# Second feed-forward pass of a hybrid pool/mLSTM block: another order of the seven products of a tile

## The chip, the cores and the metric

The kernel runs on one core of a Trainium2 chip, in one launch. The metric is the device time of the whole program in microseconds (us), lower is better. The engines are TensorE (PE), VectorE (DVE), ScalarE (ACT), GpSimd (POOL) and the DMA queue of SyncE (SP). Each works through its own list of instructions in order, and they meet at semaphores.

## The reference, cut to what matters

The reference computes two layers on an image stream x (1024 tokens in a grid of 16 x 64, width 1024) and a context stream (256 tokens). Layer 0 mixes by pooling, layer 1 by an mLSTM. The part that the change touches is the feed-forward network of layer 1 on x:

```
fx = _conv_ffn(_modulate(x, norm_g[i, 2], sh2, sc2), ffn_w_in[i], ...)

def _conv_ffn(h, w_in, conv_w, conv_b, w_out, grid):
    u, g = jnp.split(h @ w_in, 2, axis=-1)      # 1024 -> 2 x 2816
    g = _dwconv_grid(g, conv_w, conv_b, grid)   # depthwise 3x3 on the grid
    return (jax.nn.silu(g) * u) @ w_out         # 2816 -> 1024
```

Everything is float32. A product is made of three matmuls on a high and a low part of each operand (high x high, low x high, high x low).

## The kernel before, in words

The hidden width of 2816 is cut into 22 tiles of 128 channels. For a tile the kernel needs the gate g and the value u, each 128 channels x 1024 tokens, which are held as two halves of 512 tokens. The input has 1024 channels, which are two halves as well. Computed directly that is 8 block products. From tile 2 on the kernel does it with 7, by sums and differences of weight parts (`s1` to `s4`, made by POOL) and of input parts (`t1` to `t4`, made once, before tile 2). Tiles 0 and 1 are computed directly (`plain`).

A block product (`product`, L1364) is 4 x 3 matmuls of 128 x 512. Its result goes to one PSUM bank (L123): `g1`, `s2`, `s3`, `u2` go to bank A, `s1` and `s4` to bank B, `g2` to bank C. Only `g1`, `g2` and `s1` clear their bank; the others add to what stands there, after another engine has read the state in between:

- ACT copies bank A after `g1` (`keep_a`, L2217), bank B after `s1` (into `fprod`, L2222), bank A after `s2` (`keep_b`, L2225) and bank A after `u2` (into `fprod`, L2195).
- DVE adds for the gate's first half (`gate_first_half`, L2896, needs `g2`), for its second half (`gate_second`, L2882, needs `s4`) and for the value's second half (`up_second`, L2888, reads bank A after `s3`). `u2` adds to bank A after this read.

The order of the seven products on PE, and of the weight parts that ACT and POOL make for them, is `ORDER` (L118): g1, s1, s2, s4, s3, g2, u2. Tile 2 ("third") and tile 21 ("last") use `GATE_FIRST` (L117) instead. Behind the products of tile j PE computes `down` (L1463) of tile j-1: 48 matmuls of 128 x 512 with the output weights, which DVE adds into `y_x` (`f_add`, L2912).

On DVE a tile is `f_tile` (L2915): 8 taps of the convolution of tile j-1 (`f_taps`, L2859), `gate_second(j)`, the product of gate and value of tile j-1 (`f_gate`, L2867, needs ACT's silu, L2200), `up_second(j)`, `gate_first_half(j)`, `f_add(j-1)`. Tiles 3 to 12 run in a hardware loop, 13 to 20 are written out. In tiles 14 to 19 (`mod_half`) DVE also computes a piece of the modulation of layer 1, in two parts of two instructions each (`last_mod_part`, L2368 and L2371): one part behind `up_second`, one behind `gate_first_half`. They read `modh` and `macc_x` in SBUF and write `macc_x`.

Each weight part has a high half made by ACT (`part_high`, L2080, in a tile's list on ACT for the next tile) and a low half made by POOL (`part_low`, L3112). POOL also makes the sums of weight parts (`part_sum`, L3102), the low half of the output weights (`out_low`, L3118; high half `out_high`, L2092) and the low half of the gated values (`gated_low`, L3123; high half `gated_high`, L2207). The weights of tile j+1 arrive by one DMA (`halves_in`, L686), which SP issues when all seven low halves of tile j are made.

Ahead of tile 2 lies a start-up. PE computes the plain tiles 0 and 1 (L1381), first for the tokens 0 to 511 and then for 512 to 1023. Meanwhile DVE normalizes the second token half (`pre_half`, L2538 and L2546, which makes the low halves of x12 and x22), and POOL makes `out_low(0)` and then the values and low halves of `t1` to `t4` (L3143) with the weight parts of tile 2 between them.

Of the kernel before, what the change touches and what calls it, by code (L numbers as in the profile page):

```python
# [108 lines left out]
KH = KT // 2  # L109
# [7 lines left out]
GATE_FIRST = ("g1", "g2", "s1", "s2", "s4", "s3", "u2")  # L117
ORDER = ("g1", "s1", "s2", "s4", "s3", "g2", "u2")  # L118
MADE_THIRD = ("s1", "g1", "g2", "u2", "s2", "s4", "s3")
# [7 lines left out]
SUM_STEPS = (11, 12, 14, 15, 17, 18, 20, 21)  # L127
PLAIN_UP = ((1, 1), (5, 4))
THIRD_SLOT = {"g1": "g1", "g2": "g2", "u2": "u2", "s1": "s4", "s4": "s1", "s2": "s3", "s3": "s2"}
# [27 lines left out]
def build(nc, a):  # L157
    with ExitStack() as ctx:
# [351 lines left out]
        def _(sp):  # L510
# [193 lines left out]
            out_in(0)  # L704
            sp.wait_ge(sem("c_shifted"), SECOND["c_shifted"] + 4)
            sp.wait_ge(sem("pool_low"), SECOND["pool_low"] + 2)
# [27 lines left out]
        def _(pe):  # L734
# [685 lines left out]
            def third_first():  # L1420

                pe.wait_ge(sem("act_moved"), 2 * 4 + SECOND["act_moved"])
                pe.wait_ge(sem("tap_done"), SECOND["tap_done"] + 8)
                for name in ("g1", "g2"):
                    product(name, 2 * 7 + (SECOND["lo_in"] + made_at(True, name)), True)

            def products(j, third=False, last=False):
# [12 lines left out]
                if last:  # L1440
                    pe.wait_ge(sem("mod1_done"), FT)
                    product("g2", made("g2"))
                pe.wait_ge(sem("dve_moved"), j * 3 + (summed - 2))
                if third:
# [11 lines left out]
                product("s3", made("s3"), third)  # L1456
                if not (third or last):
                    pe.wait_ge(sem("dve_moved"), j * 3 + summed)
                    product("g2", made("g2"))
                pe.wait_ge(sem("dve_moved"), j * 3 + (summed + (3 if third or last else 2)))  # L1460
                product("u2", made("u2"), third)
# [17 lines left out]
            third_first()  # L1479
            pe.wait_ge(sem("act_moved"), PLAIN_MOVED + 3)  # L1480
            down(0, 0, True)
# [57 lines left out]
        def _(act):  # L1539
# [604 lines left out]
            for d in range(KT):  # L2144
                keep(posts["x_mlstm"], 3, d)
                if d == 3:
                    plain_moved(0, 0)
            half_deviation("q", 3)
            part_high("s1", 2, True)
            for d in range(KH):  # L2150
                high1(d)
            plain_moved(1, 0)
            act.wait_ge(sem("x_out1"), 32 * KT)
            for k in range(KH):
                high1(KH + k)
                act.activation(x12_at[:, k, :], res_h[:, k, :], ACT.Identity, bias=shift(1, 1, "x", k)).then_inc(sem("c_shifted"), 1)
            out_high(0)
            for k in range(KH):
                act.wait_ge(sem("pre_lo"), lows["x_pre2b"] + 12 + k + 1)
                act.activation(x22_at[:, k, :], x22_at[:, k, :], ACT.Identity, bias=shift(1, 1, "x", KH + k)).then_inc(sem("c_shifted"), 1)  # L2160
            plain_moved(0, 1)
            plain_gate(0)
            for k in (0, 2):
                act.wait_ge(sem("pool_low"), SECOND["pool_low"] + 1 + k // 2)
                pair_high("t1", k, x_val["t1"])
            for name in ("g1", "g2", "u2"):
                part_high(name, 2, True)
            for k in range(KH):
                act.activation(x21_at[:, k, :], x21_at[:, k, :], ACT.Identity, bias=shift(1, 1, "x", KH + k)).then_inc(sem("c_shifted"), 1)
            for k in (0, 2):  # L2170
                act.wait_ge(sem("pool_low"), SECOND["pool_low"] + 3 + k // 2)
                pair_high("t2", k, x_val["t2"])
            act.wait_ge(sem("tap_done"), SECOND["tap_done"] + 8)
            act.activation(acc[:], acc[:], ACT.Silu).then_inc(sem("silu_done"), 1)
            plain_moved(1, 1)
            act.wait_ge(sem("a_done"), SECOND["a_done"] + 1)
            act.activation(fa_hi[:], fprod[:, 0, :], ACT.Copy).then_inc(sem("a_hi_ready"), 1)
            for k in (0, 2):
                act.wait_ge(sem("pool_low"), SECOND["pool_low"] + 5 + k // 2)
                pair_high("t4", k, x21_at)  # L2180
            for k in (0, 2):
                act.wait_ge(sem("pool_low"), SECOND["pool_low"] + 7 + k // 2)
                pair_high("t3", k, x_val["t3"])
            plain_gate(1)
            for name in ("s2", "s4", "s3"):
                part_high(name, 2, True)

            def finish(j, par, gate_first=False):

                cv = fcv[:, j + FT, :]  # L2190
                act.wait_ge(sem("dve_moved"), j * 3 + (SECOND["dve_moved"] + (2 if gate_first else 3)))
                act.wait_ge(sem("a_done"), j + SECOND["a_done"])
                act.activation(acc[:], bank(BANK_G, TX), ACT.Identity, bias=cv[:, 9:10], scale=cv[:, 4:5]).then_inc(sem("acc_ready"), 1)
                act.wait_ge(sem("w_in_used"), j * 7 + (SECOND["w_in_used"] + 7))
                act.activation(fprod[:, par, 0:TH], ps[:, BANK_A, :], ACT.Copy).then_inc(sem("act_moved"), 1)  # L2195
# [13 lines left out]
            def tile(j, par, gate_first=False, last=False):  # L2209

                def done(name):

                    act.wait_ge(sem("w_in_used"), j * 7 + (SECOND["w_in_used"] + done_at(gate_first, name)))

                done("g1")
                act.wait_ge(sem("dve_moved"), j * 3 + SECOND["dve_moved"])
                act.activation(keep_a[:], ps[:, BANK_A, :], ACT.Copy).then_inc(sem("act_moved"), 1)  # L2217
                if not last:
                    part_high("g1", j + 1)
                out_high(j - 1)  # L2220
                done("s1")
                act.activation(fprod[:, par, TH:TX], ps[:, BANK_B, :], ACT.Copy).then_inc(sem("act_moved"), 1)  # L2222
                done("s2")
                act.wait_ge(sem("dve_moved"), j * 3 + (SECOND["dve_moved"] - 2))
                act.activation(keep_b[:], ps[:, BANK_A, :], ACT.Copy).then_inc(sem("act_moved"), 1)  # L2225
                if not last:
                    part_high("s1", j + 1)
# [7 lines left out]
                if not last:  # L2235
                    for name in ("s3", "g2", "u2"):
                        part_high(name, j + 1)
# [19 lines left out]
        def _(dve):  # L2257
# [657 lines left out]
            def f_tile(j, par, mod_half=None):  # L2915

                f_taps(j - 1)
                gate_second(j)
                f_gate(j - 1, 1 - par)
                up_second(j, par)  # L2920
                if mod_half is not None:
                    last_mod_part(mod_half, 0)
                gate_first_half(j)
                if mod_half is not None:
# [71 lines left out]
        def _(pool):  # L2996
# [128 lines left out]
            def parts(j, par):  # L3125

                part_low("g1", j)
                out_low(j - 2)
                part_sum("s1", j)
                part_sum("s2", j)  # L3130
# [6 lines left out]
                part_low("s3", j)  # L3137
                part_low("g2", j)
                part_low("u2", j)
# [17 lines left out]
            for k in (0, 2):  # L3157
                pool.wait_ge(sem("pool_low"), SECOND["pool_low"] + 1 + k // 2)
                pool.wait_ge(sem("c_shifted"), SECOND["c_shifted"] + 4 + k + 2)
                moved(x_val["t2"][:, k:k + 2, :], x22_at[:, k:k + 2], x_val["t1"][:, k:k + 2, :])  # L3160
# [130 lines left out]
```

## Time and profile before

| what | value |
|---|---|
| median of 3 runs | 2462.0 us (2458.42 to 2465.99) |
| the profiled execution's own time | 2460.98 us |
| its span | 2459.0 us |
| mean granted TensorE clock | 0.983 |
| busy: PE, PE weight load, DVE, ACT, POOL | 96%, 78%, 68%, 33%, 36% |
| chain that ended last: PE, DVE, ACT | 86%, 5%, 3% |

The second pass takes the stretch from about 1725 to 2420 us. The seven-product tiles begin at 1776. "Busy" of PE counts modelled ends of matmuls, which overlap; the distance from one start to the next tells more than the duration of one. The clock column is the granted share of TensorE's full clock.

### The profile page before, as it was taken

How to read it: one execution, taken by the hardware profiler on the slowest of the kernel's cores; microseconds unless marked ns; L12 is line 12 of the kernel's file. 1: busy time of each engine (PE TensorE's matmuls, PEld its weight loads, DVE VectorE, ACT ScalarE, POOL GpSimd, SP SyncE). 2: the span in 40 equal slices, each digit the busy share in tenths (PEclk: the TensorE clock that was granted, in tenths of full speed). 3: DMA queues.
4: the chain of work that ended last, by engine and by line, in shares of the span. 5: the costliest groups of instructions: out<-in, count | busy, mean ns of one | idle time of the engine just before them, and what ended most of it. 6: DMA issues, size and time to landing. Idle time of an engine off the chain costs nothing.

```text
span 2459.0 us, 35945 instructions
## 1 busy us (share of the span) xinstructions
PE 2355.0 (96%) x13630; PEld 1927.7 (78%) x13630; DVE 1665.1 (68%) x2156; ACT 815.3 (33%) x1186; POOL 892.6 (36%) x448
## 2 busy tenths in 40 slices
PE   7989999999999999999999998889979999999996
PEld 5557777777778778999889997767758888888884
DVE  4477888888888875553454306723657777889986
ACT  3642111211112125563443333333623333333332
POOL 0012121212212125663322005630576666666653
PEclk9999999999999999999999999989989999999998
DMA  8651212221122144653121238711211111111113
GB/s 345 231 197 77 81 47 85 85 85 51 76 85 85 74 182 154 224 180 112 55 75 59 71 108 221 226 52 69 69 44 59 52 51 51 51 60 68 68 43 137
DMA packets 106688, 255.08 MB, mean 104 GB/s; under 512 B 8928, under 2 KB 62816, under 8 KB 92128
## 3 DMA queue, kind: packets, MB, share of 16 engines
q1 hardware_dynamic: 89024, 228.56, 26.9%
q10 hardware_dynamic: 17568, 25.17, 2.8%
q8 instruction: 69, 1.13, 0.2%
q14 instruction: 27, 0.22, 0.0%
HBM read 223.68 MB, written 30.02 MB: 103 GB/s over the span
## 4 chain that ended last, share of the span: by engine, by line
PE 86%; DVE 5%; ACT 3%; DMA 2%; POOL 2%; issue 2%; SPq 0%; ACTq 0%; DVEq 0%; POOLq 0%
PE ps L737 18%; PE ps L738 17%; PE ps L739 17%; PE ps L1371 5%; PE ps L1373 5%; PE ps L1372 5%; PE ps L1123 2%; PE ps L1125 2%; PE ps L1124 2%; PE ps L1276 1%; PE ps L839 1%; PE ps L774 1%; PE ps L872 1%; PE ps L1014 1%; PE ps L790 1%
## 5 line engine op out<-in xcount | busy, mean ns | idle before, releaser
L3000 POOL TENSOR_TENSOR w_lo<-raw,w_hi 128x2048 fp32r<-128x2048 f32 x57 | 266.8, 4681 | 654.9 <-ACT w_hi L1646 294.2
L737 PE MATMUL ps<-hx_hi,w_hi 128*128 128x512 f32 x848 | 338.6, 399 | 2.4 <-ACT mix_out_c L1800 1.0
L738 PE MATMUL ps<-hx_hi,w_lo 128*128 128x512 f32 x848 | 331.8, 391 | 0.0
L739 PE MATMUL ps<-hx_lo,w_hi 128*128 128x512 f32 x848 | 331.6, 391 | 0.0
L2407 DVE TENSOR_TENSOR y_x<-y_x,ps 128x1024 f32<-128x1024 f32 x176 | 214.7, 1221 | 61.7 <-PE ps L739 56.1
L2389 DVE SCALAR_TENSOR_TENSOR acc<-ps,fcv,acc 128x945 f32<-128x945 f32 (+2 forms) x176 | 215.0, 1222 | 37.2 <-ACT acc L1690 16.1
L2912 DVE TENSOR_TENSOR y_x<-y_x,ps 128x512 f32<-128x512 f32 x304 | 206.9, 687 | 40.0 <-PE ps L739 40.0
L2859 DVE SCALAR_TENSOR_TENSOR acc<-ps,fcv,acc 128x945 f32<-128x945 f32 (+2 forms) x176 | 215.0, 1222 | 18.9 <-ACT acc L2104 4.9
L737 PEld LDWEIGHTS ps<-hx_hi,w_hi 128*128 128x128 f32 x848 | 160.0, 189 | 40.4 <-DVE hx_lo L2546 2.5
L739 PEld LDWEIGHTS ps<-hx_lo,w_hi 128*128 128x128 f32 x848 | 160.0, 189 | 34.2
L738 PEld LDWEIGHTS ps<-hx_hi,w_lo 128*128 128x128 f32 x848 | 160.1, 189 | 30.7
L3011 POOL TENSOR_TENSOR a_lo<-prod,a_hi 128x1024 fp32r<-128x1024 f32 x22 | 52.9, 2404 | 316.9 <-ACT a_hi L1708 316.9
L2358 DVE SCALAR_TENSOR_TENSOR macc<-modw,c_pad,macc 128x256 f32<-128x256 f32 x280 | 155.5, 628 | 0.0
L1123 PE MATMUL ps<-w_hi,hx_hi 128*128 128x256 f32 x512 | 146.1, 285 | 4.0 <-ACT stage L1927 4.0
L737 PE MATMUL ps<-a_hi,w_hi 128*128 128x512 f32 x352 | 145.3, 413 | 2.5 <-DVE y_x L2407 1.1
L1125 PE MATMUL ps<-w_hi,hx_lo 128*128 128x256 f32 x512 | 145.6, 284 | 0.0
L1124 PE MATMUL ps<-w_lo,hx_hi 128*128 128x256 f32 x512 | 145.5, 284 | 0.0
L737 PE MATMUL ps<-fa_hi,fw_hi 128*128 128x512 f32 x352 | 140.3, 399 | 5.0 <-DVE acc L2859 4.2
L738 PE MATMUL ps<-fa_hi,fw_lo 128*128 128x512 f32 x352 | 138.6, 394 | 0.0
L739 PE MATMUL ps<-fa_lo,fw_hi 128*128 128x512 f32 x352 | 138.5, 394 | 0.0
L738 PE MATMUL ps<-a_hi,w_lo 128*128 128x512 f32 x352 | 138.0, 392 | 0.0
L739 PE MATMUL ps<-a_lo,w_hi 128*128 128x512 f32 x352 | 137.9, 392 | 0.0
(413 smaller groups left out, 5617.5 us busy)
## 6 DMA issues: line engine op xcount, KB each, us to landing
raw<-in_ffn_w SPq DMA_DIRECT2D x44, 1024.0 KB, 6.6
modw<-in_modw SPq DMA_DIRECT2D x48, 512.0 KB, 7.1
raw<-in_ffn_w SPq DMA_DIRECT2D x44, 512.0 KB, 6.2
f_raw<-in_ffn_w SPq DMA_DIRECT2D x22, 1024.0 KB, 5.0
modw<-in_modw SPq DMA_DIRECT2D x21, 1024.0 KB, 4.8
raw<-in_mlstm_w SPq DMA_DIRECT2D x14, 1024.0 KB, 5.5
fw_raw<-in_ffn_w SPq DMA_DIRECT2D x22, 512.0 KB, 3.7
vch<-v_scr SPq DMA_DIRECT2D x18, 512.0 KB, 4.4
```

The lines of the kernel that those rows point to most:

```text
L737: pe.matmul(out, whi, hhi, start=first, stop=False)
L738: pe.matmul(out, wlo, hhi, start=False, stop=False)
L739: return pe.matmul(out, whi, hlo, start=False, stop=last)
L1123: pe.matmul(out, hi[:, k, t0:t0 + CH], wcol(0, k, 0, 2), start=first, stop=False)
L1124: pe.matmul(out, hi[:, k, t0:t0 + CH], wcol(1, k, 0, 2), start=False, stop=False)
L1125: return pe.matmul(out, lo[:, k, t0:t0 + CH], wcol(0, k, 0, 2), start=False, stop=last)
L2358: ins = dve.scalar_tensor_tensor(macc[:, x, :], modw1[:, k, :], c_pad[:, k, x:x + 1], macc[:, x, :], ALU.mult, ALU.add)
L2389: dve.scalar_tensor_tensor(out, src, cv[:, t:t + 1], out, ALU.mult, ALU.add).then_inc(sem("tap_done"), 1)
L2407: dve.tensor_tensor(y[:, d, :], y[:, d, :], bank(4 + 2 * (d % 2), p.T), ALU.add).then_inc(sem("y_added"), 1)
L2859: dve.scalar_tensor_tensor(out, src, cv[:, t:t + 1], out, ALU.mult, ALU.add).then_inc(sem("tap_done"), 1)
L2912: ins = dve.tensor_tensor(y, y, ps[:, BANK_Y + n % 3, :], ALU.add)
L3000: pool.tensor_tensor(w_lo[:, slot, 0:2048], raw[:, slot, 0:2048], w_hi[:, slot, 0:2048].bitcast(F32), ALU.subtract)\
```

## The change

All tiles use the order `GATE_FIRST`: g1, g2, s1, s2, s4, s3, u2. On DVE the order in a tile becomes `gate_first_half(j)`, `f_gate(j-1)`, `gate_second(j)`, `up_second(j)`; in tiles 14 to 19 the first part of the modulation comes between `gate_second` and `up_second`, the second behind `up_second`. ACT and POOL split the part `g2` right behind `g1`.

In the start-up ACT's list is reordered: one small Silu ahead of the second token half, `out_high(0)` moved forward, the shifts of x22 among the last high halves, `plain_gate(0)` ahead of `plain_moved(0, 1)` and of the x12 shifts. One PSUM bank of plain tile 1 moves from 4 to 6, so that `g1` and `g2` of tile 2 wait no longer for ACT's four copies of the plain tiles; `down(0)` waits for the fourth one. In tiles 2 and 3 ACT's bank copies stand between its weight splits rather than behind all of them. The diff, less the parts that only move lines of ACT's start-up:

```diff
-ORDER = ("g1", "s1", "s2", "s4", "s3", "g2", "u2")
+ORDER = GATE_FIRST
...
-PLAIN_UP = ((1, 1), (5, 4))
+PLAIN_UP = ((1, 1), (5, 6))
...
             def third_first():
 
-                pe.wait_ge(sem("act_moved"), 2 * 4 + SECOND["act_moved"])
                 pe.wait_ge(sem("tap_done"), SECOND["tap_done"] + 8)
...
+                if not third:
+                    pe.wait_ge(sem("dve_moved"), j * 3 + summed)
                     product("g2", made("g2"))
-                pe.wait_ge(sem("dve_moved"), j * 3 + (summed - 2))
+                pe.wait_ge(sem("dve_moved"), j * 3 + (summed - 1))
...
                 product("s3", made("s3"), third)
-                if not (third or last):
-                    pe.wait_ge(sem("dve_moved"), j * 3 + summed)
-                    product("g2", made("g2"))
-                pe.wait_ge(sem("dve_moved"), j * 3 + (summed + (3 if third or last else 2)))
+                pe.wait_ge(sem("dve_moved"), j * 3 + (summed + 3))
                 product("u2", made("u2"), third)
...
-            pe.wait_ge(sem("act_moved"), PLAIN_MOVED + 3)
+            pe.wait_ge(sem("act_moved"), PLAIN_MOVED + 4)
             down(0, 0, True)
...
+            act.activation(rstd_h["p", 3][:, 0:1], prmc(PM_EPS), ACT.Silu)
             part_high("s1", 2, True)
             for d in range(KH):
                 high1(d)
+            out_high(0)
             plain_moved(1, 0)
             act.wait_ge(sem("x_out1"), 32 * KT)
+
+            def second_shifted(k):
+
+                act.wait_ge(sem("pre_lo"), lows["x_pre2b"] + 12 + k + 1)
+                act.activation(x22_at[:, k, :], x22_at[:, k, :], ACT.Identity, ...)
+
             for k in range(KH):
                 high1(KH + k)
+                if k:
+                    second_shifted(k - 1)
+            second_shifted(KH - 1)
+            plain_gate(0)
+            plain_moved(0, 1)
...
+                third = gate_first and not last
                 done("g1")
                 act.wait_ge(sem("dve_moved"), j * 3 + SECOND["dve_moved"])
                 act.activation(keep_a[:], ps[:, BANK_A, :], ACT.Copy).then_inc(sem("act_moved"), 1)
-                if not last:
+                if third:
+                    part_high("s4", j, True)
+                elif not last:
                     part_high("g1", j + 1)
-                out_high(j - 1)
+                if not third:
+                    out_high(j - 1)
+                if not third and not last:
+                    part_high("g2", j + 1)
                 done("s1")
                 act.activation(fprod[:, par, TH:TX], ps[:, BANK_B, :], ACT.Copy).then_inc(sem("act_moved"), 1)
                 done("s2")
-                act.wait_ge(sem("dve_moved"), j * 3 + (SECOND["dve_moved"] - 2))
+                act.wait_ge(sem("dve_moved"), j * 3 + (SECOND["dve_moved"] - 1))
                 act.activation(keep_b[:], ps[:, BANK_A, :], ACT.Copy).then_inc(sem("act_moved"), 1)
+                if third:
+                    part_high("s3", j, True)
+                    part_high("g1", j + 1)
+                    out_high(j - 1)
+                    part_high("g2", j + 1)
                 if not last:
                     part_high("s1", j + 1)
                 silu(j - 1)
...
                 f_taps(j - 1)
-                gate_second(j)
+                gate_first_half(j, True)
                 f_gate(j - 1, 1 - par)
-                up_second(j, par)
+                gate_second(j, True)
                 if mod_half is not None:
                     last_mod_part(mod_half, 0)
-                gate_first_half(j)
+                up_second(j, par, True)
                 if mod_half is not None:
                     last_mod_part(mod_half, 1)
                 f_add(j - 1)
...
                 part_low("g1", j)
                 out_low(j - 2)
+                part_low("g2", j)
                 part_sum("s1", j)
...
                 part_low("s3", j)
-                part_low("g2", j)
                 part_low("u2", j)
```

## Rows read from the trace of the kernel before

**Rows 1.** Busy time by stretch: PE, PEld, DVE, ACT, POOL, clock, DMA.
```profile
1795.00:1825.00 30.00, 15.79 (x48) 11.69 (x48) 12.46 (x11) 6.23 (x10) 22.64 (x15) 0.77 0.15 52
1885.00:1915.00 30.00, 30.00 (x133) 24.77 (x132) 23.86 (x28) 10.42 (x16) 18.66 (x14) 1.00 0.17 53
```
**Rows 2.** Waits of PE, 1740 to 1860: us in total, times, longest.
```profile
PE ps L1371 <- ACT keep_a L2217: 7.5, 1, 7.5
PE ps L1371 <- ACT fprod L2222: 4.1, 1, 4.1
PE ps L1371 <- ACT fprod L2097: 3.9, 1, 3.9
```
**Rows 3.** Timeline of tile 21, PE and DVE: start, us, engine [idle before, releaser].
```profile
2400.15 0.39 PE L1371 MATMUL ps<-t_hi,p_s_hi 128*128 128x512 f32 x1
2401.77 0.50 PE L1371 MATMUL ps<-t_hi,p_u_hi 128*128 128x512 f32 x1 [0.78 <-DVE fprod L2888]
2402.57 0.40 PE L1371 MATMUL ps<-t_hi,p_u_hi 128*128 128x512 f32 x1
...
2401.03 0.69 DVE L2888 TENSOR_TENSOR fprod<-fprod,ps 128x512 f32<-128x512 f32 x1 [2.02 <-PE ps L1373]
```
**Rows 4.** Timeline of tile 6, in the loop: PE, ACT, POOL.
```profile
1932.51 0.39 PE L1371 MATMUL ps<-x_hi,p_g_hi 128*128 128x512 f32 x1
1935.23 0.39 PE L1371 MATMUL ps<-t_hi,p_s_hi 128*128 128x512 f32 x1
...
1941.03 0.60 ACT L2225 ACTIVATE keep_b<-ps 128x512 f32<-128x512 f32 x1 [2.27 <-PE ps L1373]
...
1947.91 2.40 POOL L3123 TENSOR_TENSOR fa_lo<-fprod,fa_hi 128x1024 fp32r<-128x1024 f32 x1 [2.33 <-ACT fa_hi L2207]
```
**Rows 5.** Timeline of tile 15, its first matmul at 2202.81: DVE, ACT, POOL.
```profile
2214.76 2.22 DVE L2867 TENSOR_TENSOR fprod<-acc,fprod 128x1024 f32<-128x1024 f32 x1
2217.49 1.06 DVE L2371 SCALAR_TENSOR_TENSOR macc_x<-modh,c_pad,macc_x 128x256 f32<-128x256 f32 x2
2219.44 0.70 DVE L2896 TENSOR_TENSOR ps<-keep_a,ps 128x512 f32<-128x512 f32 x1 [0.88 <-PE ps L1373]
...
2213.66 1.06 ACT L2200 ACTIVATE acc<-acc 128x1024 f32<-128x1024 f32 x1 [0.91 <-DVE acc L2859]
...
2214.61 1.28 POOL L3102 TENSOR_TENSOR p_s_val<-f_raw,p_s_val 128x512 f32<-128x512 f32 x1
2218.22 2.59 POOL L3123 TENSOR_TENSOR fa_lo<-fprod,fa_hi 128x1024 fp32r<-128x1024 f32 x1 [2.33 <-ACT fa_hi L2207]
```
**Rows 6.** Timeline of the start-up: DVE, ACT, POOL, SP, PE.
```profile
1748.02 1.60 DVE L2546 SCALAR_TENSOR_TENSOR x_lo<-res_h,modt,x_hi 128x512 fp32r<-128x512 f32 x1
1756.80 1.63 DVE L2546 SCALAR_TENSOR_TENSOR x_lo<-y_x,modt,x_hi 128x512 fp32r<-128x512 f32 x2
...
1752.27 0.58 ACT L2097 ACTIVATE fprod<-ps 128x512 f32<-128x512 f32 x1
1758.16 1.04 ACT L2092 ACTIVATE fw_hi<-fw_raw 128x1024 fp32r<-128x1024 f32 x1
1822.52 1.04 ACT L2200 ACTIVATE acc<-acc 128x1024 f32<-128x1024 f32 x1
...
1747.78 1.29 POOL L3112 TENSOR_TENSOR p_s_lo<-p_s_val,p_s_hi 128x512 fp32r<-128x512 f32 x1
1798.13 4.68 POOL L3143 TENSOR_TENSOR t_lo<-t_val,t_hi 128x1024 fp32r<-128x1024 f32 x2
1820.67 1.28 POOL L3102 TENSOR_TENSOR p_s_val<-f_raw 128x512 f32<-128x512 f32 x1 [3.50 <-PE ps L1373]
...
1807.45 0.34 SPq L686 DMA_DIRECT2D f_raw<-in_ffn_w  x1
...
1827.06 0.80 PE L1371 MATMUL ps<-t_hi,p_u_hi 128*128 128x512 f32 x1 [3.67 <-DVE fprod L2888]
1831.50 0.39 PE L737 MATMUL ps<-fa_hi,fw_hi 128*128 128x512 f32 x1
```

More of the change, by code:

```diff
@@ L704, in _ @@
             out_in(0)
-            sp.wait_ge(sem("c_shifted"), SECOND["c_shifted"] + 4)
+            sp.wait_ge(sem("c_shifted"), SECOND["c_shifted"] + 8)
             sp.wait_ge(sem("pool_low"), SECOND["pool_low"] + 2)
@@ L2151, in _ @@
                 high1(d)
+            out_high(0)
             plain_moved(1, 0)
             act.wait_ge(sem("x_out1"), 32 * KT)
+            def second_shifted(k):
+                act.wait_ge(sem("pre_lo"), lows["x_pre2b"] + 12 + k + 1)
+                act.activation(x22_at[:, k, :], x22_at[:, k, :], ACT.Identity, bias=shift(1, 1, "x", KH + k)).then_inc(sem("c_shifted"), 1)
             for k in range(KH):
                 high1(KH + k)
-                act.activation(x12_at[:, k, :], res_h[:, k, :], ACT.Identity, bias=shift(1, 1, "x", k)).then_inc(sem("c_shifted"), 1)
[L2157 to L2162, printed above, removed]
+                if k:
[3 more added lines that the diff above has]
+            plain_moved(0, 1)
+            for k in range(KH):
+                act.activation(x12_at[:, k, :], res_h[:, k, :], ACT.Identity, bias=shift(1, 1, "x", k)).then_inc(sem("c_shifted"), 1)
+            for name in ("g1", "g2", "u2"):
+                part_high(name, 2, True)
             for k in (0, 2):
@@ L2165, in _ @@
                 pair_high("t1", k, x_val["t1"])
-            for name in ("g1", "g2", "u2"):
-                part_high(name, 2, True)
             for k in range(KH):
@@ L2172, in _ @@
                 pair_high("t2", k, x_val["t2"])
+            part_high("s2", 2, True)
             act.wait_ge(sem("tap_done"), SECOND["tap_done"] + 8)
@@ L2177, in _ @@
             act.activation(fa_hi[:], fprod[:, 0, :], ACT.Copy).then_inc(sem("a_hi_ready"), 1)
+            plain_gate(1)
             for k in (0, 2):
@@ L2183, in _ @@
                 pair_high("t3", k, x_val["t3"])
-            plain_gate(1)
-            for name in ("s2", "s4", "s3"):
-                part_high(name, 2, True)
             def finish(j, par, gate_first=False):
                 cv = fcv[:, j + FT, :]
-                act.wait_ge(sem("dve_moved"), j * 3 + (SECOND["dve_moved"] + (2 if gate_first else 3)))
+                act.wait_ge(sem("dve_moved"), j * 3 + (SECOND["dve_moved"] + 2))
                 act.wait_ge(sem("a_done"), j + SECOND["a_done"])
@@ L2235, in tile @@
                 if not last:
-                    for name in ("s3", "g2", "u2"):
+                    for name in ("s3", "u2"):
                         part_high(name, j + 1)
@@ L3158, in _ @@
                 pool.wait_ge(sem("pool_low"), SECOND["pool_low"] + 1 + k // 2)
-                pool.wait_ge(sem("c_shifted"), SECOND["c_shifted"] + 4 + k + 2)
+                pool.wait_ge(sem("c_shifted"), SECOND["c_shifted"] + k + 2)
                 moved(x_val["t2"][:, k:k + 2, :], x22_at[:, k:k + 2], x_val["t1"][:, k:k + 2, :])
```

## The prediction

> **What bounds the kernel now.** I read the busy time by stretch first, because the page's shares average over stages. In the running tiles PE is never idle: 133 matmuls in 30 us at full clock, with DVE at 24 and POOL at 19 of the 30 [rows 1]. So from tile 3 on nothing hides a wait of PE, and nothing but fewer or faster matmuls could shorten a tile. Around tile 2 it is otherwise: PE is busy for 15.8 of 30 us, and the clock falls to 0.77 [rows 1]. The list of PE's waits names the causes there: 3.9 us before `g1` for ACT's copies of the plain tiles, 7.5 us before `s2` for `keep_a`, 4.1 us before `s4` for ACT's copy of bank B [rows 2], and 3.7 us before `u2` for `up_second` [rows 6]. The change aims at these 19 us, which occur once. But it also changes 18 tiles that have no gap, and I price those first.
>
> **Tiles 3 to 20: a bank that is used twice in a row.** `s3` and `u2` both go to bank A, and between them DVE must read it (`up_second`). Before, `g2` stood between the two, in bank C, and its 2.72 us (1935.23 - 1932.51) [rows 4] covered the read. Now `u2` follows `s3` directly. Tile 21 already has this order, so the trace shows the price. DVE waits there 2.02 us for PE, so it isn't late, and still PE is idle for 0.78 us. From the last group of `s3` (2400.15) to the second of `u2` (2402.57) it is 2.42 us [rows 3], where two groups of three matmuls take 2 x 0.68 (a quarter of 2.72) = 1.36. The cost is 1.06 us, semaphores and refilling included.
>
> Is DVE in time in the new order too? I lay out a tile from its first matmul; products end every 2.72 us. `s2` is now fourth and done at 10.9. `keep_b` followed `s2` at 8.52 when the product ended at 8.16 [rows 4], so it is now at 11.2; then come the split of `s1` (0.5) and the silu at 12.2. The silu now stands behind `keep_b` and not behind the taps. DVE's `f_gate` can start 1.10 later (2213.66 to 2214.76) [rows 5], at 13.3. There POOL is in its way. In tile 15 `f_gate` took 2.22 us, against 1.1 without company, while a POOL instruction ran from 2214.61 to 2215.89 [rows 5]: it waited for that one's end and then ran. Of DVE's instructions those with two operands in SBUF show this; `gate_first_half`, which reads one from PSUM, took its normal 0.70 in the middle of a POOL instruction [rows 5]. So `f_gate` runs from 13.7 to 14.8, behind POOL's low half of `s1`, `gate_second` until 15.5, and `s3` ends at 16.3. DVE is free in time. `down(j-1)` needs `gated_low`, at about 18.5, and starts after 20. No other wait grows. In the 12 tiles without modulation (3 to 13, and 20) the cost is 12 x 1.06 = 12.7 us.
>
> **Tiles 14 to 19: the modulation in front of the read.** Here two more instructions stand between `gate_second` and `up_second`. Uncontended they take 1.06 us together [rows 5], until 16.5, and would cost next to nothing more. But both operands are in SBUF, and POOL is busy. Its sum for `s4` (1.28) waits for the lock that `f_gate` holds and runs from 14.8 to 16.1, so the first of the two runs at 16.1 to 16.6. `gated_low` is ready 1.24 us after `f_gate` ends (2216.98 to 2218.22) [rows 5], also at 16.1, and takes its turn at 16.6 for 2.40 [rows 4]. The second instruction waits for the first one's result, hence comes behind it, from 19.0 to 19.5. `up_second` (0.69 [rows 3]) ends at 20.1, `u2` starts 3.8 us late. After 3.67 us of idle time PE ran `u2` of tile 2 in 4.44 us (1827.06 to 1831.50) [rows 6] and not in 2.72, at the lower clock: 1.7 more. Per tile 5.5, and 6 x 5.5 = 33 us. From below it is 6 x 1.06 = 6.4 (both instructions slip in before `gated_low`); from above 6.7 a tile, 40 us (`f_gate` or the first part misses one more POOL instruction of 1.28). I take 33, because in every contended row the two engines take turns.
>
> The Trainium skill, page "SBUF — State Buffer", section "Who interferes with whom", gives this as a rule: a DVE instruction with two SBUF inputs and a POOL instruction that reads SBUF exclude each other for a whole instruction, whoever started first. By that rule the trace agrees (2.22 against 1.1 us). It also says that a `tensor_scalar` can take the same pair of ports, which no row here shows. That matters, because in tiles 14, 16 and 18 the first instruction of the part is a `tensor_scalar` (L2368). By the page these tiles behave as the others.
>
> If it is not blocked, it runs at 15.5 while POOL works, and the second instruction gets the place before `gated_low`. Then three of the six tiles cost 1.06 and not 5.5.
>
> **The start-up.** The end of it is the start of `u2` of tile 2, 1827.06. The chain to it: SP issues the weights of tile 3 at 1807.45, when the last low half of tile 2 is made, and ACT does the silu at 1822.52, since that stands behind the split of `s1` of tile 3; `u2` comes 4.54 later. Of the 19.6 us POOL waited 3.50 for PE [rows 6], which goes, and the low half of `g2` comes in (1.3): 17.4. So what decides is when tile 2's low halves are ready. `s3`'s high half is now behind `keep_b`, and that behind `s2`, which needs POOL's low half of `t2` (made until 1802.8) [rows 6].
> From below: `out_high(0)` moves from 1758.16 to 1752.27 [rows 6], POOL's list starts 5.9 earlier, loses about 2.4 of it (my estimate from ACT's list) waiting for ACT's shifts of x21, and is 3.5 early: `s2` from 1799.5 to 1802.2, copy, split and low half 2.8, issue at 1805.0, `u2` at 1822.4. That is 4.7 us gained, with `g1` starting about when the plain products end.
> From above: POOL's early instructions (2.4 each) now fall among the four low halves that DVE makes for x22 until 1758.4 [rows 6], which have two SBUF operands too. One of these took 1.60 and not 0.74 when it met a POOL instruction at 1747.78 [rows 6]. Taking turns, they end at 1765.5. PE's last plain block starts 5.5 late, with it the taps of tile 0 and `down(0)`, and the low half of `t2` is done at 1805.2. `s2` starts cold (4.4, as `u2` of tile 2 above), the issue is at 1812.7, `u2` at 1830.1, and it runs 0.4 longer: 3.4 us lost. I take 3 us lost, nearer to this end, because the contended rows all show the turns. The removed stalls are real, but the same POOL list is late behind them. The early Silu only moves a table load into idle time of ACT.
>
> **The sum.** 12.7 + 33 + 3 = 48.7 on the profiled execution's 2461.0 gives 2509.7. The median of the runs stands 1.0 above that execution: 2510.7, so 2510.
>
> **The rivals.**
> 1. The modulation hides: all 18 tiles cost 1.06, 19.1 us, with the start-up between -4.7 and +3: 2477 to 2484. For it: the order of the turns hangs on differences of about 0.5 us. Against it: the first instruction and `gated_low` become ready in the same tenth. Three of six (the `tensor_scalar`): 2510 - 3 x 4.4 = 2497.
> 2. Faster. The only gain is in the start-up: bank copies no longer behind splits that wait for POOL and DMA. Worth 4.7, or about 6 if the clock also holds in `u2`. It decides from the point where the running tiles cost less than 0.26 us each (4.7 / 18), that is where PE hardly notices the read between `s3` and `u2`. Then it is 2457. Against it stands tile 21's 1.06, with a DVE that was waiting.
> 3. Slower still: the first part and `f_gate` both lose a turn, or POOL's later list delays `down`: 2520 to 2530.
>
> **Chances.** The forecast 0.50 (own range 2500 to 2518), three of six 0.12, rival 1 0.23, rival 3 0.06, rival 2 0.06, and 0.03 for a draw in which the start-up gains more than I see. The range runs from 2477 to 2519. Within 0.3% (7 us) can't be told from no change. Faster 0.06, same 0.04, slower 0.90.
>
> **What would show it.** Right: in the loop tiles PE is idle 0.8 us before each `u2`, released by `up_second`, and tiles start 31.1 us apart instead of 30.0; in tiles 14 to 19 the idle time is about 3.6 us, the second L2371 starts behind `gated_low`, the clock dips at `u2`, and tiles take 35.5 us. In the start-up, L2546 rows of up to 3 us between 1754 and 1766, PE idle three times for 1.6 us in the last plain blocks, and the DMA of tile 3's weights later than 1807. Wrong: tiles 14 to 19 with the same 0.8 us as the others (rival 1); `u2` of tile 2 before 1823 (the start-up gained); or loop tiles still 30.0 us apart, which would upset the whole sum.

## The result, and the profile after

| | before, same chip | after |
|---|---|---|
| median | 2460.94 us (4 runs) | 2501.52 us (2496.94 to 2502.04, 4 runs) |
| ratio | | 1.017, interval 1.0156 to 1.0184 |
| profiled execution, its span | 2461.0, 2459.0 us | 2502.0, 2499.9 us |
| mean granted TensorE clock | 0.983 | 0.981 |

The change makes the kernel 40.6 us slower. I read the waits of PE first, as before. This is the list for the second pass of the kernel after (1735 to 2460 us): time in total, times, longest.

```profile
PE ps L1371 <- DVE fprod L2904: 36.1, 20, 7.3
PE ps L1371 <- POOL t_lo L3159: 5.5, 2, 4.5
PE ps L737 <- DVE acc L2875: 4.2, 1, 4.2
PE ps L1371 <- issue: 4.0, 1, 4.0
PE ps L1381 <- DVE x_lo L2562: 3.8, 4, 1.1
```

The three waits for ACT's bank copies [rows 2] are gone. PE now stands 4.0 us in front of `s2` of tile 2 and 4.5 in front of `s3`; both are waits for POOL's low halves (for the first, "issue", the list names no releaser, but `s2` starts at 1800.72 and the low half of `t2` is done at 1800.62). The other 1.0 us of the POOL line was there before. New are 3.8 us in the last plain blocks, for DVE's low halves. The largest cause has 36.1 us: `up_second` (L2904 here), which frees bank A for `u2`. It holds PE up in 20 tiles, once in each; in the kernel before it did so twice, in tiles 2 and 21, for 4.5 us. Tile 2 has 7.3 of the 36.1. Which tiles take how much is in the table of stretches: tile 3, tile 15, then tiles 4 to 13, which have no modulation, and the six tiles 14 to 19, which have it. Columns: PE, PEld, DVE, ACT and POOL busy, clock, DMA share, GB/s.

```profile
1841.39:1872.57 31.18, 30.32 (x133) 24.71 (x132) 23.98 (x29) 10.53 (x15) 19.50 (x13) 1.00 0.15 51
2219.29:2254.20 34.91, 31.92 (x133) 25.84 (x132) 29.42 (x33) 10.30 (x15) 19.98 (x13) 0.95 0.17 60
1872.57:2184.38 311.81, 303.25 (x1321) 247.07 (x1320) 239.97 (x281) 104.56 (x150) 194.66 (x130) 1.00 0.15 51
2184.39:2394.56 210.17, 192.36 (x793) 155.76 (x792) 176.42 (x193) 61.96 (x90) 119.70 (x78) 0.94 0.17 57
```

The same 133 matmuls that took 30.0 us [rows 1] take 31.18 us in a plain loop tile, and PE is now idle in it. Ten more such tiles take 311.81. The six with modulation take 210.17, or 35.03 each, at a mean clock of 0.94.

**A loop tile** (tile 5), PE and DVE, to be held against tile 21 in [rows 3]:

```profile
1919.96 0.39 PE L1373 MATMUL ps<-t_lo,p_s_hi 128*128 128x512 f32 x1
1921.20 0.49 PE L1371 MATMUL ps<-t_hi,p_u_hi 128*128 128x512 f32 x1 [0.86 <-DVE fprod L2904]
...
1918.61 0.68 DVE L2898 TENSOR_TENSOR ps<-keep_b,ps 128x512 f32<-128x512 f32 x1
1920.39 0.69 DVE L2904 TENSOR_TENSOR fprod<-fprod,ps 128x512 f32<-128x512 f32 x1 [1.10 <-PE ps L1373]
```

`up_second` has 1.10 us of slack ahead of it: DVE waits for PE. PE then waits 0.86 us for DVE. It is a handover through one bank, and no engine is late.

**A tile with modulation** (tile 15, first matmul at 2219.29), DVE, POOL and PE:

```profile
2232.62 1.59 DVE L2883 TENSOR_TENSOR fprod<-acc,fprod 128x1024 f32<-128x1024 f32 x1 [1.68 <-ACT acc L2205]
2234.14 0.68 DVE L2898 TENSOR_TENSOR ps<-keep_b,ps 128x512 f32<-128x512 f32 x1
2234.74 3.41 DVE L2387 SCALAR_TENSOR_TENSOR macc_x<-modh,c_pad,macc_x 128x256 f32<-128x256 f32 x2
2238.07 0.67 DVE L2904 TENSOR_TENSOR fprod<-fprod,ps 128x512 f32<-128x512 f32 x1
...
2233.33 2.05 POOL L3118 TENSOR_TENSOR p_s_val<-f_raw,p_s_val 128x512 f32<-128x512 f32 x1 [0.19 <-PE ps L1373]
2235.47 2.40 POOL L3139 TENSOR_TENSOR fa_lo<-fprod,fa_hi 128x1024 fp32r<-128x1024 f32 x1
...
2238.88 0.56 PE L1371 MATMUL ps<-t_hi,p_u_hi 128*128 128x512 f32 x1 [2.99 <-DVE fprod L2904]
```

The two instructions of L2387 took 1.06 us in [rows 5] and take 3.41 here. The chain of waits splits them: the first ended at 2235.67, 0.3 behind POOL's sum (2235.38). The second was begun by 2235.76, but DVE's next instruction came only at 2238.07, behind POOL's `fa_lo` (the instruction that the prediction calls `gated_low`), which ended at 2237.87. `up_second` stands behind both on DVE.

**The start-up**, POOL, SP, ACT, PE and DVE, beside [rows 6]:

```profile
1762.19 2.41 POOL L3159 TENSOR_TENSOR t_val<-y_x,t_val 128x1024 f32<-128x1024 f32 x1 [1.45 <-ACT y_x L2158]
1767.09 2.57 POOL L3128 TENSOR_TENSOR p_g_lo<-f_raw,p_g_hi 128x512 fp32r<-128x512 f32 x2 [2.49 <-ACT p_g_hi L2078]
1771.32 4.79 POOL L3159 TENSOR_TENSOR y_x<-y_x,t_val 128x1024 f32<-128x1024 f32 x2 [1.67 <-ACT y_x L2175]
1795.90 4.72 POOL L3159 TENSOR_TENSOR t_lo<-t_val,t_hi 128x1024 fp32r<-128x1024 f32 x2
...
1808.71 0.34 SPq L686 DMA_DIRECT2D f_raw<-in_ffn_w  x1
...
1821.58 1.04 ACT L2205 ACTIVATE acc<-acc 128x1024 f32<-128x1024 f32 x1
...
1773.76 0.40 PE L1371 MATMUL ps<-x_hi,p_g_hi 128*128 128x512 f32 x1
1800.72 0.77 PE L1371 MATMUL ps<-t_hi,p_s_hi 128*128 128x512 f32 x1 [3.99 <-issue]
1813.23 0.77 PE L1371 MATMUL ps<-t_hi,p_s_hi 128*128 128x512 f32 x1 [4.47 <-POOL t_lo L3159]
1825.98 0.79 PE L1371 MATMUL ps<-t_hi,p_u_hi 128*128 128x512 f32 x1 [7.29 <-DVE fprod L2904]
...
1743.00 1.40 DVE L2554 SCALAR_TENSOR_TENSOR res_h<-y_x,der,ps 128x512 f32<-128x512 f32 x2 [2.47 <-PE ps L881]
1756.29 5.00 DVE L2562 SCALAR_TENSOR_TENSOR x_lo<-y_x,modt,x_hi 128x512 fp32r<-128x512 f32 x2
```

All work ahead of the second pass is untouched, yet its end falls at different times in different executions. So I measure the start-up from its first DVE instruction, the one released by L881: 1743.00 here, and 1746.48 in the kernel before. From there to `u2` of tile 2 it is 82.98 us after and 80.58 before (1827.06 in [rows 6]); to the first matmul of tile 3 98.39 and 95.93. Up to tile 3 the kernel after lost 2.5 us.

**Where the 40.9 us of the spans are.** Eleven steps from tile 3 to 14 at 1.15 (31.18 - 30.03) are 12.65, tile 20 adds 1.15 (32.44, with the 1.26 that it has over a loop tile in both kernels), six tiles with modulation at 5.0 are 30.0, the start-up 2.5: 46.3. Against it stand 3.5 us by which this execution entered the second pass earlier, and 1.8 us in the tail, where the last `down` ran longer at a lower clock in the profiled execution of the kernel before (0.50 from 2415 to 2420) and not here. Neither of these is a term of the change. The point of entry moves by itself between the traces of the experiments below. In all nine other traces, those with the old order among them, the last `down` runs as it does here: 29.2 to 29.3 us, where the kernel before has 31.3.

### The profile page after: what moved, and what is told of

It reads as the page before. It is cut to its first block, busy times and chain, and to the rows that moved or that the text cites. A ratio compares the mean times of both kernels' runs of the same rounds, so it can differ in the third digit from the quotient of the medians.

```text
span 2499.9 us, 35974 instructions
## 1 busy us (share of the span) xinstructions
PE 2365.2 (95%) x13630; PEld 1927.9 (77%) x13630; DVE 1680.8 (67%) x2156; ACT 812.4 (32%) x1187; POOL 908.3 (36%) x448
## 4 chain that ended last, share of the span: by engine, by line
PE 84%; DVE 6%; ACT 4%; issue 3%; DMA 2%; POOL 2%; SPq 0%; ACTq 0%; DVEq 0%; POOLq 0%
PE ps L737 18%; PE ps L739 16%; PE ps L738 16%; PE ps L1371 5%; PE ps L1373 5%; PE ps L1372 5%; PE ps L1123 2%; PE ps L1124 2%; PE ps L1125 2%; PE ps L839 1%; PE ps L1276 1%; PE ps L774 1%; PE ps L872 1%; PE ps L1014 1%; PE ps L790 1%
## 5 line engine op out<-in xcount | busy, mean ns | idle before, releaser
L2928 DVE TENSOR_TENSOR y_x<-y_x,ps 128x512 f32<-128x512 f32 x304 | 206.9, 687 | 71.9 <-PE ps L739 71.9
L2405 DVE SCALAR_TENSOR_TENSOR acc<-ps,fcv,acc 128x945 f32<-128x945 f32 (+2 forms) x176 | 215.0, 1222 | 37.6 <-ACT acc L1688 16.4
L738 PEld LDWEIGHTS ps<-hx_hi,w_lo 128*128 128x128 f32 x848 | 160.2, 189 | 30.7
```

The costliest lines, as they stand in the source:

```text
L738: pe.matmul(out, wlo, hhi, start=False, stop=False)
L2405: dve.scalar_tensor_tensor(out, src, cv[:, t:t + 1], out, ALU.mult, ALU.add).then_inc(sem("tap_done"), 1)
L2928: ins = dve.tensor_tensor(y, y, ps[:, BANK_Y + n % 3, :], ALU.add)
```

## The experiments

All are compared by ratio with the kernel before on the same chip. Its median was 2459.24 us beside the first four and 2458.26 us beside the last four. "Span" is that of the profiled execution.

**1. The two halves of the change alone.** `e1_start_only` keeps the new start-up and puts the running order back:

```diff
-ORDER = GATE_FIRST
+ORDER = ("g1", "s1", "s2", "s4", "s3", "g2", "u2")
...
-                    for name in ("s3", "u2"):
+                    for name in ("s3", "g2", "u2"):
```

> Only the start-up half of the change: ACT's reordered list, the moved PSUM bank and the bank copies between the splits of tile 2; the running tiles keep the order of before. My theory (the start-up gains nothing, because POOL's instructions now alternate with DVE's low halves and the weights of tile 3 are asked for later): 1 to 3 us slower than before, so 2462 to 2464 where before is 2461. u2 of tile 2 starts about 2.4 us later, counted from DVE's first instruction on the second token half, than in the kernel before; the running tiles are 30.03 us apart. Rival (the start-up gains as its removed waits of 19 us suggest, and the running tiles hide it): 4 us or more faster than before, at most 2457.

Measured: 2458.17 us, ratio 0.9994 (0.9985 to 1.0004), 10 runs; span 2458.3. Loop tiles are 30.04 us apart. From the anchor, `u2` of tile 2 starts after 81.69 us, 1.1 later than before where 2.4 was expected, and tile 3 after 97.79, 1.9 later.

`e2_order_only` keeps the new running order (bodies of `products`, `tile`, `f_tile` and `parts`) and puts the start-up back:

```diff
-PLAIN_UP = ((1, 1), (5, 6))
+PLAIN_UP = ((1, 1), (5, 4))
...
-            act.activation(rstd_h["p", 3][:, 0:1], prmc(PM_EPS), ACT.Silu)
...
-                third = gate_first and not last
+                third = False
```

> Only the other half: the start-up of before, the new order of the seven products in all tiles and in the lists of ACT, DVE and POOL. My theory: the loss is all here. 12 tiles at +1.15 us and 6 at +5.0 us are +44 us, so 2502 to 2508 where before is 2461, and above the full change by 0 to 3 us less what its start-up loses. Rival (the loss needs the start-up's shifts too): below 2490.

Measured: 2499.44 us, ratio 1.0165 (1.0148 to 1.0182), 4 runs; span 2499.7. Loop tiles 31.18 us apart, tiles with modulation 35.25. The time is just under the 2502 to 2508 that were expected. Tile 3 starts 97.19 us behind the anchor, 1.3 later than before with the old start-up: PE's wait for ACT's copy of bank B in tile 2 grew from 4.1 to 5.1 us. So not all of the 2.5 us ahead of tile 3 is the start-up's.

So the loss is in the running tiles. The start-up is nothing that the medians can tell from zero: the interval of the first kernel reaches from 3.7 us faster to 1.0 slower. The 1.9 us of its anchored trace lie outside this interval. The trace is one execution, the interval rests on ten; where the difference lies is not shown.

**2. The modulation out of the read's way.** `e3_mod_behind` changes only DVE's order in the tiles with modulation:

```diff
+                up_second(j, par, True)
                 if mod_half is not None:
                     last_mod_part(mod_half, 0)
-                up_second(j, par, True)
```

> The full change, but in tiles 14 to 19 both parts of the modulation stand behind the read of bank A (up_second), none in front. Theory (the first part in front of the read loses a turn to POOL's gated_low and PE waits for it): these six tiles fall from 35.0 to 31.2 us, and the total by 6 x 3.85 = 23 us, from 2501.5 to 2478. Rival (the modulation costs time wherever it stands, since DVE has more to do in these tiles): they stay near 35 us and the total within 5 us of 2501.

Measured: 2491.81 us (2486.03 to 2493.3), ratio 1.0137 (1.012 to 1.0154), 4 runs; span 2483.5. The gain on the whole change is real, 8 us by the ratios and 14 by this trace (6 x (35.03 - 32.68); the profiled execution was the fastest of the four, and what the other three had more is not in any trace). Some 23 were expected. PE's waits in the six tiles (2183 to 2380 us) tell why:

```profile
PE ps L737 <- DVE y_x L2928: 7.3, 6, 1.3
PE ps L1371 <- DVE fprod L2904: 5.1, 6, 0.9
```

The wait in front of `u2` fell from 3.0 to 0.85 us a tile, as it should. The first line is new: `down` waits for its bank. DVE in tile 15 of that kernel:

```profile
2231.56 0.69 DVE L2904 TENSOR_TENSOR fprod<-fprod,ps 128x512 f32<-128x512 f32 x1 [1.10 <-PE ps L1373]
2232.17 5.89 DVE L2387 SCALAR_TENSOR_TENSOR macc_x<-modh,c_pad,macc_x 128x256 f32<-128x256 f32 x4
2237.98 5.14 DVE L2928 TENSOR_TENSOR y_x<-y_x,ps 128x512 f32<-128x512 f32 x8
```

All four modulation instructions now stand behind `up_second` and ahead of `f_add` (L2928) in one piece, take 5.89 us in POOL's company, and `down`, which runs right behind `u2`, meets the banks that `f_add` has not yet read. The tiles are 32.68 us apart, not 31.2. The turns had moved, and were not gone.

`e4_mod_one` moves only one of the two instructions:

```diff
-                for k in range(KH * h + 2 * e, KH * h + 2 * e + 2):
+                for k in range(KH * h + e, KH * h + (4 if e else 1)):
```

> The full change, but only the first of the two instructions of the modulation's first part stands in front of the read; the other three of the tile stand behind it. Theory of turns: the first instruction gets its turn before gated_low, and only the second was caught behind it. With one instruction DVE reads bank A at about 16.7 us of the tile and not at 19.2, PE waits 0.9 to 1.3 us: tiles of 31.2 to 31.6 us, and the total falls by 20 to 23 us, to 2479 to 2482. Rival (each instruction in front costs its share of the time): half of the extra goes, tiles of 33.1 us, total near 2490.

Measured: 2482.39 us, ratio 1.0094 (1.0077 to 1.011), 4 runs; span 2481.0. The tiles are 31.38 us apart, and PE's list for 2187 to 2376 us has a single line:

```profile
PE ps L1371 <- DVE fprod L2904: 5.1, 6, 0.9
```

DVE and POOL in tile 15 of it:

```profile
2234.32 0.92 DVE L2387 SCALAR_TENSOR_TENSOR macc_x<-modh,c_pad,macc_x 128x256 f32<-128x256 f32 x1
2235.51 0.69 DVE L2904 TENSOR_TENSOR fprod<-fprod,ps 128x512 f32<-128x512 f32 x1 [0.27 <-PE ps L1373]
2236.11 4.52 DVE L2387 SCALAR_TENSOR_TENSOR macc_x<-modh,c_pad,macc_x 128x256 f32<-128x256 f32 x3
...
2235.05 2.43 POOL L3139 TENSOR_TENSOR fa_lo<-fprod,fa_hi 128x1024 fp32r<-128x1024 f32 x1
```

One instruction still goes in ahead of POOL's `fa_lo`, and `up_second`, which reads PSUM, then runs in the middle of it. So nearly all that a tile with modulation lost above the others (35.03 - 31.18 = 3.85 us) was the second instruction's missed turn, with the dip of the clock behind it: 35.03 - 31.38 = 3.65 us a tile, 21.9 us in six. By the two ratios it is 18.7, a little under the 20 to 23 expected. The rival's 33.1 us a tile is refuted. With one instruction in front this is also 9 us faster than with none in front, since the three behind now delay nothing that PE waits for.

**3. The bank.** `e5_u2_bank` sends `u2` of the running tiles to bank C, which is free since `g2` is now early. It leaves out the sum that bank A holds, so the value's first half is `u2`'s own product alone: the kernel serves to time the wait, it does not compute the reference. Not shown in the cut are the flag that clears bank C, ACT's copy from C and a wait ahead of `g1`:

```diff
-                out = ps[:, PRODUCT_BANK[name], :]
+                out = ps[:, BANK_C if other else PRODUCT_BANK[name], :]
...
-                pe.wait_ge(sem("dve_moved"), j * 3 + (summed + 3))
-                product("u2", made("u2"), third)
+                pe.wait_ge(sem("dve_moved"), j * 3 + (summed + (1 if other else 3)))
+                product("u2", made("u2"), third, other)
```

> The full change, but in tiles 3 to 20 u2 goes into bank C instead of bank A, so it no longer follows s3 in the same bank and doesn't wait for DVE's read. It leaves out the sum that bank A holds: the value's first half gets u2's own product alone. Theory (the bubble is the read between two uses of one bank): no idle time before u2, the loop tiles are 30.0 us apart, as before the change; tiles 14 to 19 lose the 3 us wait as well, but DVE's late instructions there may cost down(j-1) up to 1.5 us: 30 to 31.6 us. Total 2457 to 2467. Rival (having g2 early, or the lists of ACT and POOL in their new order, costs PE time by itself): loop tiles stay near 31.2 us and the total near 2500.

Measured: 2466.9 us, ratio 1.0032 (1.002 to 1.0045), 6 runs; span 2462.6. PE's whole list for the running tiles, 1841 to 2389 us:

```profile
PE ps L737 <- DVE y_x L2930: 6.3, 6, 1.1
```

No wait for `up_second` is left, the loop tiles are back at 30.04 us, and the same order costs nothing in them. What remains is a distance of 31.4 us in each of the six tiles with modulation, where the missed turn is still there (3.46 us for the two instructions in this trace too) but now delays only `f_add`. 6 x 1.37 = 8.2 us, and 8.6 were measured (7.9 by the ratio), though this trace too has tile 3 2.3 us later than before. So the order by itself costs the loop tiles nothing; its price is the wait for the bank's reader.

**4. Why the start-up gains nothing.** `e6_late_out` is `e1_start_only` with `out_high(0)` moved back behind the shifts of x22, where POOL and DVE no longer meet:

```diff
-            out_high(0)
             plain_moved(1, 0)
...
             second_shifted(KH - 1)
+            out_high(0)
             plain_gate(0)
```

> The start-up half alone, but ACT's out_high(0) stands behind the shifts of x22, so POOL starts its list later and doesn't meet DVE's four low halves of x22. Theory (the two engines take turns, and this ate the start-up's gain): PE's four waits for x_lo (0.5 and 3 x 1.1 us) disappear, g1 of tile 2 starts 3 us earlier counted from DVE's first instruction on this token half, and the low half of t2 is ready no later than with out_high(0) early. u2 of tile 2 starts 1 to 2 us earlier than in the start-up half alone: total 1 to 2 us less. Rival (POOL's earlier start is worth what it costs): t2's low half is ready 3 us later, and u2 with it.

Measured: 2458.5 us, ratio 0.9999 (0.9989 to 1.0008), 10 runs; span 2453.9. DVE and POOL in it:

```profile
1752.18 1.62 DVE L2560 SCALAR_TENSOR_TENSOR x_lo<-y_x,modt,x_hi 128x512 fp32r<-128x512 f32 x2
...
1794.40 4.68 POOL L3157 TENSOR_TENSOR t_lo<-t_val,t_hi 128x1024 fp32r<-128x1024 f32 x2
...
1768.87 0.47 PE L1371 MATMUL ps<-x_hi,p_g_hi 128*128 128x512 f32 x1 [1.03 <-POOL p_g_lo L3126]
1823.20 0.80 PE L1371 MATMUL ps<-t_hi,p_u_hi 128*128 128x512 f32 x1 [5.98 <-DVE fprod L2902]
```

The contention is gone (the last two low halves take 1.62 us together, not 5.00), and the first `g1` starts 27.0 us behind the anchor (1741.85) instead of 30.7 in the first experiment. But POOL's last `t2` low half is done after 57.2 us (1799.08) against 57.6, and `u2` starts after 81.4 against 81.7. Expected were 1 to 2 us at `u2`, and the rival's 3 us later did not come either. Nearly four microseconds gained on PE at the front are worth 0.3 at the end, because POOL's list, and not PE, sets the end. The two kernels' medians can't be told apart.

**5. What ends the start-up.** `e7_early_silu` is `e1_start_only` with the silu of tile 1 (and the high half that follows it) right behind `keep_b` and `s3`'s split in tile 2, and not behind the split of tile 3's `s1`, which waits for a DMA and for POOL. POOL's low half for it (`gated_low`) goes first in tile 3's list:

```diff
                 if third:
                     part_high("s3", j, True)
+                    silu(j - 1)
+                    gated_high(j - 1, 1 - par)
                     part_high("g1", j + 1)
                     out_high(j - 1)
...
             def parts(j, par, early=False):
+                if early:
+                    gated_low(j - 2, par)
                 part_low("g1", j)
```

> The start-up half alone, and in tile 2 ACT does the silu of tile 1 and its gated high half right behind the split of s3, ahead of the splits that wait for the weights of tile 3; POOL makes gated_low(1) ahead of tile 3's parts. Theory (u2 of tile 2 waits 7 us only because the silu stands behind the split of s1 of tile 3, which waits for DMA and POOL): u2 starts 1 us after s3 ends, about 6 to 7 us earlier, and the total is 5 to 8 us below the kernel before: 2451 to 2455. Rival (something else is as late: down(1) or g1 of tile 3 waits in its place): the total stays within 2 us of 2459.

Measured: 2452.28 us (2451.0 to 2454.08), ratio 0.998 (0.9969 to 0.999), 9 runs; span 2452.1. ACT, DVE and PE in it, its anchor being 1746.24:

```profile
1810.46 1.05 ACT L2206 ACTIVATE acc<-acc 128x1024 f32<-128x1024 f32 x1
...
1823.12 0.69 DVE L2906 TENSOR_TENSOR fprod<-fprod,ps 128x512 f32<-128x512 f32 x1 [9.50 <-PE ps L1373]
...
1817.63 0.76 PE L1371 MATMUL ps<-t_hi,p_s_hi 128*128 128x512 f32 x1 [5.28 <-POOL t_lo L3164]
1823.86 0.51 PE L1371 MATMUL ps<-t_hi,p_u_hi 128*128 128x512 f32 x1 [0.78 <-DVE fprod L2906]
```

DVE is now 9.50 us early for `up_second`, PE's wait before `u2` falls from 7.1 to 0.78, and `u2` starts 77.6 us behind the anchor (80.58 before). Tile 3 starts after 91.36: 4.6 us ahead of the kernel before and 6.4 ahead of the first experiment. It beats the kernel before by 0.2%, with an interval that leaves no change out. Next late is `s3` of tile 2, whose wait for POOL's `t3` grew from 4.47 to 5.28.

`e8_early_late` joins the last two edits.

> The two previous edits together. If both theories hold it is the fastest, 1 to 2 us below the one with the early silu alone: 2450 to 2454. If out_high(0) early is better for POOL's list, it is above that one.

Measured: 2452.5 us (2450.44 to 2457.32), ratio 0.9983 (0.9974 to 0.9993), 10 runs; span 2448.8. Tile 3 starts 90.98 us behind the anchor, 0.4 earlier than without the second edit. That is again what PE's early `g1` is worth, and too little to see in the medians: the 1 to 2 us below `e7_early_silu` that were expected did not come. Held against `e6_late_out`, from which only the early silu sets it apart, on the same chip, it is 6.0 us faster (2458.5 to 2452.5), and its tile 3 starts 6.4 earlier (97.4 to 91.0).

## Why the prediction came out as it did

It forecast 2510 us (range 2477 to 2519), slower; 2501.5 was measured, inside the range, 8.5 below. Step by step:

- **A loop tile, 1.06 us: right, a little small.** It was 1.15, from 0.86 us of idle time before `u2` where tile 21 had 0.78 [rows 3]. Over 12 tiles 13.8 us for 12.7. Taking a later tile that already had the order as the sample for the rest gave the term to 0.1 us, and the bank experiment shows that its cause is the wait for the bank's reader: with `u2` elsewhere it is 0.
- **A tile with modulation, 5.5 us: the mechanism right, the size 0.5 too large.** The forecast order of turns is the one in the trace, instruction by instruction: `f_gate` at +13.3, POOL's sum until +16.1, one modulation instruction, `fa_lo`, the other, `up_second`. Forecast and measured end of `up_second`: +20.1 and +19.45. The 0.6 us between them is at the change of turns: I let `fa_lo` start only when the first modulation instruction was through, at +16.6, and end at +19.0; its row starts at +16.2, while that instruction ends (+16.4), and it is done at +18.6. The idle time was 2.95 and not 3.6. The clock's part was right on average: `u2` took 4.43 us in tile 15 (2238.88 to 2243.31), as the 4.44 in [rows 6], and 4.22 to 5.28 in the six tiles (2.84 in a loop tile), with a granted clock of 0.50 to 0.65. In all 30.0 us for 33. That tiles 14, 16 and 18, whose first instruction is a `tensor_scalar`, behave as the others was the other open question of this step. They do: the idle time before `u2` is 2.94 to 2.99 us in all six. This refutes rival 1 and its three-of-six form. Two small readings were off and changed nothing: `f_gate` without company takes 1.22 to 1.27 us in the kernel before, not 1.1, and 5.5 + 1.28 is 6.8, not 6.7.
- **The start-up, 3 us lost: 2.5 in the trace, and invisible in the medians.** The forecast chain and the measured one, both counted from the anchor: L2546's low halves done 19.0 and 18.3; `t2` low half done 58.7 and 57.6; weights of tile 3 issued 66.2 and 65.7; `u2` 83.6 and 83.0. Two details were off. The first is how POOL comes to be late. From the start of `out_low(0)` to the end of `t2`'s low half POOL took 50.7 us (1749.90 to 1800.62) where the kernel before took 43.5 (1759.28 to 1802.81), and of these 7.2 us more, 5.6 are waits for ACT (1.45, 2.49 and 1.67), whose shifts of x22 wait in turn for DVE's last low half (1761.29). I had put these waits at 2.4 in the favourable case. At most 1.6 are turns of POOL's own with DVE. The second is PE, which idled once for 0.45 us and three times for 1.1, not three times for 1.6. And the two halves alone put tile 3 back by 1.9 (start-up) and 1.3 us (order), so the 2.5 are not shown to be the start-up's alone. The sentence that "the removed stalls are real, but the same POOL list is late behind them" is what the late-`out_high` experiment shows.
- **The sum.** 46.3 us in the trace for 48.7. The other 5.3 us between the two spans are no term of the change: the sum was laid on one execution, of 2461.0 us, which happened to enter the second pass late and to run its last `down` at a low clock. `e2_order_only`, whose code up to tile 2 is that of the kernel before, entered it at 1742.57 and not 1746.48. A sum that is made on one execution carries that execution's luck. But this explains two spans and not the medians. They too are only 40.6 us apart (38.4 to 45.3 by the interval), and the medians of the kernel before beside the experiments, 2459.24 and 2458.26 us, stand no more than 2.7 below the 2461.0 of that execution. Why the medians differ by less than the terms add up to stays open. So of the 8.5 us of the miss 2.4 are terms that were too large, and nearly all the rest is this difference, for which the forecast has no term.
- **What I did not see.** I priced the start-up's end as given once POOL's lows were done, and took the silu's place behind tile 3's `s1` split as it stood. Moving this one instruction, with the two that make the gated halves behind it, is worth more (6.4 us) than all that the start-up half rearranged.

## What to carry to other kernels

When two products in a row go to the same bank, their reader's round trip is on PE's path in each tile, even with the reader waiting ready: 1.15 us here for a read of 0.69. Put another bank's product between them, or, where the second does not need the sum in the bank (here `u2` does), give it another bank. Before you put instructions that must share something with another engine ahead of an instruction that frees a bank, count their turns: each may have to wait a whole turn, and that, not the busy time, is the price (1.06 us of work became 3.41 here). Moving all of them behind is not best by itself: with none, one and two in front the tiles took 32.68, 31.38 and 35.03 us.

Before removing an engine's stalls in a start-up, follow the chain that ends it. Three stalls of up to 7.5 us were removed here, and tile 3 came 2.5 us later; one silu that stood behind the split of another tile's weights brought it 6.4 us forward.

## What the runs showed of the hardware

A DVE `tensor_scalar` with its data in SBUF is held up by POOL as the two-operand forms are. In tile 14 of the kernel after, DVE and POOL:

```profile
2199.84 0.78 DVE L2384 TENSOR_SCALAR macc_x<-modh,c_pad 128x256 f32<-128x256 f32 x1
2200.73 2.47 DVE L2387 SCALAR_TENSOR_TENSOR macc_x<-modh,c_pad,macc_x 128x256 f32<-128x256 f32 x1
...
2198.43 2.04 POOL L3118 TENSOR_TENSOR p_s_val<-f_raw,p_s_val 128x512 f32<-128x512 f32 x1 [0.19 <-PE ps L1373]
2200.57 2.35 POOL L3139 TENSOR_TENSOR fa_lo<-fprod,fa_hi 128x1024 fp32r<-128x1024 f32 x1
```

It took 0.78 us, ending 0.15 behind POOL's sum, and 0.78 to 0.79 in all three tiles that have it. The same instruction in the kernel before, with POOL idle (0.34 in all three):

```profile
2187.47 0.34 DVE L2368 TENSOR_SCALAR macc_x<-modh,c_pad 128x256 f32<-128x256 f32 x1
```

The Trainium skill, page "SBUF — State Buffer", section "Who interferes with whom", says that a `tensor_scalar` can take the shared ports too; by that the trace agrees.

The clock fell after idle times of only 2.9 to 3.0 us: the stretch from 2308.40 to 2312.50 had a granted clock of 0.50, the lower of its two levels (1.2 GHz), in a pass in which the loop before ran at 1.00 (2.4 GHz). After the 0.86 us of the loop tiles it did not fall. In the tiles with modulation the dip costs about half as much again as the idle time: 35.03 us is 30.03 plus 3.3 (2.95 idle and the refilling of 0.3 that the loop tiles show) plus 1.7.

The time at which the work ahead of the second token half's normalization ends, the same instructions in all these kernels but for one small Silu of ACT, differs by up to 5.7 us between profiled executions (1740.78 to 1746.48). Differences of 2 us in a chain are to be read from an anchor next to it, not from the span.
